# Splitting the experts' down product into one-pass products in a decoder step on one core

## The reference

```python
def expert_block(args):
    tok, e = args
    xb = h[tok]
    return (jax.nn.silu(xb @ w_gate[e]) * (xb @ w_up[e])) @ w_down[e]
```

## Time and profile before

| what | value |
|---|---|
| median of 3 runs | 2600.66 us (2597.71 to 2602.58) |
| the profiled execution's own time | 2591.6 us |
| its span, first to last instruction | 2589.8 us |
| experts: first `gate_up` to the last block's `gate_up` | 2175.20 to 2516.23 us, 31 periods |
| PE, DVE, ACT, POOL busy in the span | 91%, 51%, 39%, 25% |
| mean granted TensorE clock | 0.951 |

### The profile page before, as it was taken

How to read it: one execution, slowest core, us unless ns; L and a number is a source line. 1 busy time by engine, 2 the same in 40 slices (tenths; PEclk the granted TensorE clock), 3 DMA queues, 4 the chain that set the end, 5 groups by cost and what they waited for, 6 DMA issues and landing times. The chain is left out here.

```text
span 2589.8 us, 46955 instructions
## 1 busy us (share of the span) xinstructions
PE 2358.8 (91%) x18273; PEld 1804.9 (70%) x18273; DVE 1324.3 (51%) x2529; ACT 1017.2 (39%) x2036; POOL 656.3 (25%) x716
## 2 busy tenths in 40 slices
PE   6999999999799999789999999799997995999980
PEld 6999999999788888635656556666663554666660
DVE  6365664333157777334555556344442435666655
ACT  5157751132122323314544545343441113665652
POOL 0100000011135454323333331244440111222210
PEclk9999999999879999989999999899998996999995
DMA  4222233334245353140000100467674502999865
GB/s 146 82 66 73 83 104 105 107 129 145 90 127 148 97 151 92 42 135 1 26 26 26 41 35 10 156 243 270 240 273 131 214 28 90 342 355 347 333 258 214
DMA packets 178645, 361.23 MB, mean 139 GB/s; under 512 B 36596, under 2 KB 128200, under 8 KB 157945
## 3 DMA queue, kind: packets, MB, share of 16 engines
q1 hardware_dynamic: 145609, 225.01, 25.8%
q0 software_dynamic: 32848, 133.56, 13.6%
HBM read 302.91 MB, written 72.18 MB: 145 GB/s over the span
## 5 line engine op out<-in xcount | busy, mean ns | idle before, releaser
L136 PE MATMUL pi_acc<-hT_hi,pi_w_hi 128*128 128x352 f32 (+1 forms) x1152 | 378.7, 329 | 0.0
L136 PE MATMUL pi_acc<-hT_lo,pi_w_hi 128*128 128x352 f32 (+1 forms) x1152 | 371.8, 323 | 0.0
L136 PE MATMUL pi_acc<-hT_hi,pi_w_lo 128*128 128x352 f32 (+1 forms) x1152 | 371.7, 323 | 0.0
L2791 DVE TENSOR_TENSOR ex_w_lo<-w_raw,ex_w_hi 128x512 fp32r<-128x512 f32 x256 | 160.0, 687 | 120.7 <-ACT ex_w_hi L2759 120.7
L136 PEld LDWEIGHTS pi_acc<-hT_hi,pi_w_hi 128*128 128x128 f32 x1152 | 217.6, 189 | 4.0 <-issue 3.8
L136 PEld LDWEIGHTS pi_acc<-hT_lo,pi_w_hi 128*128 128x128 f32 x1152 | 217.4, 189 | 4.0 <-issue 3.8
L136 PEld LDWEIGHTS pi_acc<-hT_hi,pi_w_lo 128*128 128x128 f32 x1152 | 217.3, 189 | 0.0
L2759 ACT CAST ex_w_hi<-w_raw 128x512 fp32r<-128x512 f32 x256 | 140.1, 617 | 100.4 <-DMA w_raw<-w_up 49.7
L1654 PE MATMUL at_sc<-at_keyT,at_qT 96*128 96x512 f32 (+5 forms) x480 | 161.1, 443 | 3.2 <-POOL at_qT L1584 2.3
L1910 ACT ACTIVATE at_p<-at_sc,at_nm 16x16 f32<-16x16 f32 (+5 forms) x144 | 100.7, 699 | 155.3 <-DVE at_nm L1773 154.2
L1771 DVE TENSOR_REDUCE at_mx<-at_sc 16x1 f32<-16x16 f32 (+5 forms) x144 | 101.3, 704 | 96.2 <-PE at_sc L1658 95.3
(11 more groups left out here) (509 smaller groups left out, 4931.0 us busy)
## 6 DMA issues: line engine op xcount, KB each, us to landing
w_raw<-w_gate SPq DMA_DIRECT2D x32, 1024.0 KB, 8.7
w_raw<-w_up SPq DMA_DIRECT2D x32, 1024.0 KB, 12.0
wd<-w_down SPq DMA_DIRECT2D x32, 1024.0 KB, 6.3
pi_piece<-w_in SPq DMA_DIRECT2D x64, 384.0 KB, 3.3
projT<-pi_xr POOLq DMA_DIRECT2D x24, 524.0 KB, 3.2
convT<-pi_yn POOLq DMA_DIRECT2D x24, 512.0 KB, 2.9
gp_heads<-convT SPq DMA_DIRECT2D x8, 1536.0 KB, 8.6
gp_zg<-projT SPq DMA_DIRECT2D x16, 512.0 KB, 5.3
```

Source lines behind the costliest of these rows:

```text
L136: last = nc.tensor.matmul(out, lhs[a], rhs[b], start=(start and i == 0), stop=(stop and i == 2))
L2791: nc.vector.tensor_tensor(w_lo[:, c, :].rearrange("p (j f) -> p j f", j=2), raw[:, i, :, c * DE:(c + 1) * DE], w_hi[:, c, :].bitcast(F32). ...
```

## The change

`w_down` is split as the other weights are. ACT casts each quarter (128x512) of `wd` to `wd_hi`, POOL subtracts to make `wd_lo`, both in double buffers; DVE splits `hT` into `hT_hi` and `hT_lo` instead of copying it; PE runs three one-pass products for each fp32 product. The w_down load of block b+1 now waits for `down_lo` of block b-1 (POOL's split) and no longer for `y_done`; PE's `down` waits for `down_lo` where it waited for `d_loaded`.

```diff
@@ buffers
-        hT = s.sb("ex_hT", [P, KE, P])
+        hT_hi, hT_lo = (s.sb(f"ex_hT_{n}", [P, KE, P], F32R) for n in ("hi", "lo"))
+        wd_hi, wd_lo = (s.sb(f"ex_wd_{n}", [P, 2, 2 * KE, BANK], F32R) for n in ("hi", "lo"))
@@ SP body
-                        sp.wait_ge(y_done, b)
+                        sp.wait_ge(down_lo, b * 2 * KE)
@@ POOL
+                def make_down_lo(b, i):
+                    for c in range(2 * KE):
+                        pool.wait_ge(down_hi, b * 2 * KE + c + 1)
+                        pool.sem_inc(gather_due, 1)
+                        nc.gpsimd.tensor_tensor(wd_lo[:, i, c, :], wd[:, i, c * BANK:(c + 1) * BANK], wd_hi[:, i, c, :].bitcast(F32), ALU.subtract).then_inc(down_lo, 1)
+
                 def body(b, i, ahead):
                     if ahead > 1:
                         gather(b + 2, i)
+                    make_down_lo(b, i)
                     if after(b, 1):
                         store(b - 1, 1 - i)
@@ PE down
-                    pe.wait_ge(d_loaded[i], (b - i) * 8 + 16)
+                    pe.wait_ge(down_lo, (b + 1) * 2 * KE)
...
-                            last = nc.tensor.matmul(yps[:, n, :], hT[:, c, :], wd[:, i, c * D + n * BANK:c * D + (n + 1) * BANK], start=(c == 0), stop=(c == KE - 1))
+                            last = split_matmul(nc, yps[:, n, :], [v[:, c, :] for v in (hT_hi, hT_lo)], [v[:, i, 2 * c + n, :] for v in (wd_hi, wd_lo)], c == 0, c == KE - 1)
@@ ACT
+                def keep_down_hi(b, i):
+                    act.wait_ge(d_loaded[i], (b - i) * 8 + 16)
+                    if after(b, 2):
+                        act.wait_ge(y_done, b - 1)
+                    for c in range(2 * KE):
+                        nc.scalar.copy(wd_hi[:, i, c, :], wd[:, i, c * BANK:(c + 1) * BANK]).then_inc(down_hi, 1)
+
                 def body(b, i, ahead):
+                    keep_down_hi(b, i)
                     if ahead:
                         keep_hi(b + 1, 1 - i)
@@ DVE body
-                    nc.vector.tensor_copy(hT[:].rearrange("p c t -> p (c t)"), hps[:, 0:DE]).then_inc(h_kept, 1)
+                    nc.vector.tensor_copy(hT_hi[:].rearrange("p c t -> p (c t)"), hps[:, 0:DE]).then_inc(h_hi, 1)
+                    dve.wait_ge(h_hi, b + 1)
+                    nc.vector.tensor_tensor(hT_lo[:].rearrange("p c t -> p (c t)"), hps[:, 0:DE], hT_hi[:].bitcast(F32).rearrange("p c t -> p (c t)"),
+                                            ALU.subtract).then_inc(h_kept, 1)
```

More of the change, by code:

```diff
@@ L2616, in experts @@
         hi_made, lo_made, used = (s.sem(f"ex_{n}") for n in ("hi_made", "lo_made", "used"))
+        down_hi, down_lo, h_hi = (s.sem(f"ex_{n}") for n in ("down_hi", "down_lo", "h_hi"))
         x_turned, x_hi, x_lo, silu_done, h_done, h_turned, h_kept, y_done, y_kept = (
```

## The result

The changed kernel takes 2677.38 us (median of 4 runs, 2673.56 to 2681.43), against 2599.18 us for the kernel before on the same chip: a ratio of 1.0307 with a 95% interval of 1.0287 to 1.0328, slower by 3%. The forecast was 2684 us with a range of 2615 to 2712. The profiled execution has a span of 2679.6 us at a mean clock of 0.932; before it was 2589.8 at 0.951.

What follows compares the result with a forecast made beforehand. PE was taken to bound the experts stage, DMA close behind; POOL's hold on DVE lengthens 31 periods from 10.82 to 13.5 us, +83 on 2591.6, 2675; runs' median 9.1 higher gives 2684 us, range 2615 to 2712.

Steps and rivals of the forecast that it cites:

- The mechanism: Experts stage: POOL's four w_down subtractions hold DVE's eight `w_lo` subtractions, on the path to the next `gate_up`; chance 0.62.
- the sum: Experts stage: 31 periods of 13.5 us instead of 10.82, +83 us.
- POOL's product: One 128x512 subtraction making `wd_lo`, taken at 1.27 us, 5.1 us for each block.
- the dear product in fp32r: Rival: POOL's subtraction takes 2.36 us each because of its output type; +207 us, 2808 us; chance 0.05.
- PE's product: One-pass product in `down`: 0.232 us each, twelve cost 2.78 us, 0.66 less for each block, buying nothing.
- ACT's wait for the up weights: Sign in the profile after: ACT no longer waits for them; before, 49.7 us in 19 blocks.
- G + 14.5 - T: Start of POOL's four products; G: start of a block's `gate_up`, T: period; at T = 13.2, G + 1.3.
- the half miss: Rival: POOL's four products split around DVE's stream; period 10.94 us, +4 us, 2604 us; chance 0.06.
- ACT's casts: Four w_down casts ahead of the eight for `w_hi`: 2.13 us, covered if the period is long.
- 7.42: Chain in us from ACT's first `w_hi` cast, through DVE's eight subtractions, `h` and `make_x_lo`, to the next `gate_up`.
- The clock: Low clock after PE's idle in some blocks, period 13.5 us; rival, low in every block: 2696 to 2706, chance 0.15.
- costs nothing: The w_down load, behind 2 MB of gate and up weights: DMA keeps ahead with a period above 9.85 us.

## Why the prediction was right, and where not

*The mechanism and the sum.* POOL holds DVE's stream, and that makes the time: shown by taking away the reads (2590) and by moving the same products behind the stream (2596). The sum was +83 us for the stage; it measured +82. POOL's product: 1.27 foreseen, 1.29 measured, so the dear product in fp32r is out. PE's product: 0.232 foreseen, 0.229 measured from start to start, and its gain buys nothing here. `w_lo` 1.2 to 1.3 us foreseen, 1.14 measured; DMA share 0.73, 0.69; ACT's wait for the up weights gone, as said.

*The size came out of two wrong halves, and that they fit so well is luck.* The prediction looked for one period that repeats: products at G + 14.5 - T, all in the stream, T = 13.2, and said against the half miss that "each block meets in the same way". They don't. By the same formula a long period puts the next products before the stream, and a short one wholly into it: T = 15.7 gives G - 1.2 (measured G - 0.5), T = 11.6 gives G + 2.9 (measured G + 5.3: `keep_y` ended 2.1 us later than in the formula, behind a `gate_up` at the low clock). So the stage swings between the two. The formula alone would not keep that up: from 15.7 it leads to 10.7, 13.5, 12.9 and stays between 12.9 and 13.5. What the trace has beyond it are ACT's casts in the long block and the low clock in the short one (both below). That these keep the swing going is a reading of the trace, and no run isolates it; in its favour, the swing goes where the products leave the stream (periods of 11.3 and 11.4 us with ScalarE's casts behind w_hi). The collision costs 10.22 - 4.91 = 5.3 us in a long block and 7.02 - 4.91 = 2.1 in a short one, 3.7 in the mean where 4.8 was summed.

*ACT's casts were not hidden.* They were put at nothing if the period is long. But in the short block `keep_y` starts at 2398.77, 11.62 past `gate_up` and not 10.15, since `gate_up` ran at the low clock (its 24 products took 7.78 us for 5.56); the four casts follow, and the next block's eight start behind them at 2401.77, G + 3.0 and not G + 0.98. With that the long block is 3.0 + 7.42 + 5.3 = 15.7. This 2.0 us in every second block makes up for the smaller collision.

*The clock* falls in some blocks, as said: in every second one, behind 5 us of idle and not 2.3. The short block is 1.66 + 7.42 + 2.1 = 11.2 for 11.6 measured; 1.66 is the first cast's start at the low clock. Of the 0.4 left, 0.33 stand ahead of `make_x_lo`: it starts 0.66 us behind `h` (2396.40), where before it was 0.33, and waits for `keep_x` (row 2397.06). `keep_x` is late because ACT's eight casts last from 2388.81 to 2395.76, 6.95 us for 4.26, waiting for PE between the first ones (0.66 us twice, then 0.39) while the clock is low.

*w_down* "costs nothing" holds in the changed kernel, because its periods are long. With VectorE's `wd_lo` it stops the gain (42.0 us of waits, 2601 us); with ScalarE's casts moved as well, that wait is gone and the time is 2585.

The Trainium skill's rule (SBUF — State Buffer, "Who interferes with whom") held in both directions: two SBUF inputs against a reading GpSimd are held (a `w_lo` of 6.00 us), beside writes alone (0.69 in the mean) and with an input in PSUM (1.22 for `make_x_lo`, as without POOL) they are not. It says that the one that issues later waits for the other's instruction. Here that is what some blocks show; in most blocks of the changed kernel, DVE waited for all the products that POOL still had to do (last section).

## What to carry to other kernels

Work that goes to GpSimd is not free because GpSimd is idle: ask which VectorE instructions with two SBUF inputs run at that time, and whether they are on the path. If they are, set a wait that puts GpSimd's reads beside other work: one wait took back the whole 3% here. When a chain's delay depends on when the last block ended, try the formula with a long and a short period before taking the one that repeats, and with those terms added that only one of the two brings on the path.

## What the runs showed of the hardware

Inside the loop of the changed kernel, a `w_lo` that meets POOL's products is held to the end of the last one: 6.00 us where all four are ahead, 2.73 where it comes during the third; with eight products, up to 9.4. It ends 0.55 us behind the last of them, even where the record shows it starting 0.43 us ahead of the first (2403.63 against 2404.06). Since a `w_lo` in the stream adds some 0.6 us, nearly all its work was done behind the burst; its start in the record doesn't show who came first. Writes between the products, with 0.19 us of no reading, did not end the hold there (6.76 us).

DVE does get in between two products elsewhere: in blocks 0, 1 and 30 of the changed kernel, which are written out outside the loop, and in most blocks of the run with POOL's products and ScalarE's casts between keep_x and keep_y. Two blocks of that run, one behind the other:

```profile
2291.07 1.23 POOL L2671 DMA_INDIRECT x_rows<-ffn_in,x_idx  x1 [0.85 <-POOL x_idx L2668]
2294.02 5.51 POOL L2691 TENSOR_TENSOR ex_wd_lo<-wd,ex_wd_hi 128x512 fp32r<-128x512 f32 x4 [1.72 <-ACT ex_wd_hi L2785]
2296.86 1.52 DVE L2808 TENSOR_TENSOR ex_w_lo<-w_raw,ex_w_hi 128x512 fp32r<-128x512 f32 x1 [0.68 <-ACT ex_w_hi L2768]
...
2303.39 1.23 POOL L2671 DMA_INDIRECT x_rows<-ffn_in,x_idx  x1 [0.85 <-POOL x_idx L2668]
2304.64 5.04 POOL L2691 TENSOR_TENSOR ex_wd_lo<-wd,ex_wd_hi 128x512 fp32r<-128x512 f32 x4
2307.18 3.06 DVE L2808 TENSOR_TENSOR ex_w_lo<-w_raw,ex_w_hi 128x512 fp32r<-128x512 f32 x1 [1.23 <-ACT ex_w_hi L2768]
```

Both `w_lo` start in POOL's third product. The first ends at 2298.38, before the burst does (2299.53), and POOL's last product takes 1.75 us for 1.29: the two engines take turns. The second ends at 2310.24, behind the burst (2309.68). What differs ahead of them is that POOL was idle for 1.72 us before the first burst, while the second starts 0.02 us behind the end of an indirect transfer's instruction. The same holds over the traces of the five kernels in which a `w_lo` meets a burst with more than its last product to come: of 122 bursts that start within 0.05 us of such an instruction's end, 121 held the `w_lo` to their end; of 26 that start 0.15 us or more behind it, none did. No run changed this alone, so it is a pattern and not a cause that is shown; it also fits the gaps between products that changed nothing, since those bursts too started directly behind the gather.
